# Scans that read ones from PSUM, and `1 - a` split between VectorE and GpSimd, in a hybrid decoder step

## The reference

```python
z = einsum('bqhd,bkhd->bhqk', q, k) * SB_HEAD_DIM ** -0.5 + bias
log_keep = where(vis, log_sigmoid(-z), 0)
after = cumsum(log_keep, reverse=True) - log_keep
a = where(vis, exp(log_sigmoid(z) + after), 0)
out = einsum('bhqk,bkhd->bqhd', a, v)
```

## Time and profile before

| | us |
|---|---|
| median of 3 runs | 2907.35 (2905.9 to 2910.66) |
| the profiled execution | 2908.15 |
| its span, first to last instruction | 2906.3 |
| TensorE busy in the span | 2503.2 |
| VectorE busy | 1422.4 |
| GpSimd busy | 1021.5 |
| ScalarE busy | 813.6 |

### The profile page before, as it was taken

How to read it: one execution, slowest core, us unless ns; L and a number is a source line. 1 busy time by engine, 2 the same in 40 slices (tenths; PEclk the granted TensorE clock), 3 DMA queues, 4 the chain that set the end, 5 groups by cost and what they waited for, 6 DMA issues and landing times. The chain is left out here.

```text
span 2906.3 us, 37872 instructions
## 1 busy us (share of the span) xinstructions
PE 2503.2 (86%) x14073; PEld 1568.7 (54%) x14073; DVE 1422.4 (49%) x1669; ACT 813.6 (28%) x1746; POOL 1021.5 (35%) x546
## 2 busy tenths in 40 slices
PE   5999899998599996999999667878888876886998
PEld 3555444443244443888888654555555554553443
DVE  1111066576100002555555319999999983442333
ACT  2222031223000001222222115656565642221110
POOL 2434010101000001435444005898898970002554
PEclk9999899999799997999999758999898998997999
DMA  5232212220522102011011121000000008994332
GB/s 155 90 96 92 47 30 45 61 60 15 93 64 70 59 31 65 27 39 43 29 43 33 46 99 64 30 30 1 30 30 1 30 1 291 330 325 164 127 127 83
DMA packets 150639, 224.91 MB, mean 77 GB/s; under 512 B 15632, under 2 KB 86241, under 8 KB 145416
## 3 DMA queue, kind: packets, MB, share of 16 engines
q1 hardware_dynamic: 150536, 223.50, 24.7%
HBM read 154.55 MB, written 68.91 MB: 77 GB/s over the span
## 5 line engine op out<-in xcount | busy, mean ns | idle before, releaser
L1561 DVE TENSOR_TENSOR_SCAN f_x<-f_x 128x2064 f32<-128x2064 f32 (+15 forms) x128 | 473.0, 3696 | 4.4
L1588 POOL TENSOR_TENSOR f_a<-f_a,f_x 128x2063 f32<-128x2063 f32 (+15 forms) x128 | 398.8, 3124 | 124.9 <-DVE f_x L1561 124.9
L629 PE MATMUL ps<-hT,wa 128*128 128x512 f32 (+1 forms) x960 | 354.4, 532 | 45.3 <-DMA wa<-w_in 45.3
L447 PE MATMUL ps<-hT,wc 128*128 128x512 f32 (+1 forms) x960 | 355.4, 532 | 12.8 <-DMA wc<-w_in 12.8
L629 PEld LDWEIGHTS ps<-hT,wa 128*128 128x128 f32 x960 | 168.7, 191 | 230.6 <-issue 185.1
L1456 PE MATMUL ps<-con,f_a 128*128 128x128 f32 x1216 | 189.7, 296 | 102.1 <-POOL f_a L1588 102.1
L447 PEld LDWEIGHTS ps<-hT,wc 128*128 128x128 f32 x960 | 169.1, 192 | 198.3 <-issue 198.3
L2010 PE MATMUL ps<-m_w,m_mT 128*128 128x512 f32 x544 | 238.1, 596 | 0.0
L321 PE MATMUL ps<-wt,hT_now 128*128 128x512 f32 x544 | 237.7, 595 | 0.0
L1511 ACT ACTIVATE f_at<-ps 128x512 f32<-128x512 f32 (+3 forms) x352 | 182.2, 539 | 197.6 <-PE ps L1456 195.2
L1456 PEld LDWEIGHTS ps<-con,f_a 128*128 128x128 f32 x1216 | 139.9, 149 | 138.7 <-POOL f_a L1588 108.7
(11 more groups left out here) (277 smaller groups left out, 3514.6 us busy)
## 6 DMA issues: line engine op xcount, KB each, us to landing
j_kp<-cache_k SPq DMA_DIRECT2D x128, 256.0 KB, 4.1
j_v<-cache_v SPq DMA_DIRECT2D x128, 256.0 KB, 4.7
chan<-y SPq DMA_DIRECT2D x12, 1088.0 KB, 6.0
chan<-ya SPq DMA_DIRECT2D x12, 1088.0 KB, 4.8
d_ld<-chan SPq DMA_DIRECT2D x16, 768.0 KB, 5.3
h_rows<-hg SPq DMA_DIRECT2D x17, 512.0 KB, 4.9
m_hh<-h_rows SPq DMA_DIRECT2D x17, 512.0 KB, 5.0
xin<-x_prompt SPq DMA_DIRECT2D x16, 512.0 KB, 4.1
```

What stands on the lines that cost most here:

```text
L447: m = pe.matmul(ps[:, ci, 0:n], wc[k][:, c, :], hT[:, c, c0:c0 + n], start=(c == 0), stop=(c == KC - 1))
L629: m = pe.matmul(ps[:, ci, 0:n], wc[k][h % 2][:, c, :], hT[:, c, c0:c0 + n], start=(c == 0), stop=(c == KC - 1))
L1561: dve.tensor_tensor_scan(dst[:, ::-1], dst[:, ::-1], dst[:, ::-1], 1.0, ALU.mult, ALU.bypass).then_inc(scanned, 1)
L1588: pool.tensor_tensor(w, w, x_at(u, h, i)[:, 1:], ALU.mult).then_inc(weighed, 1)
```

## The change

- A PSUM bank that nothing else writes (bank 7) gets a 1.0 in its first column, and `ones(n)` is that column, repeated n times. The value products move from bank 7 to bank 6.
- The transposes have two banks instead of three; `turn(t)` waits for the copy of turn t-2.
- The scan's unused operand is `ones(n)` instead of `x`, for both heads.
- The first head's `1 - a` stays on VectorE, but is a tensor_tensor: `ones(n)` minus `a`. The second head's moves to GpSimd, as the tensor_scalar that it was, in GpSimd's list ahead of the row's two products. It waits for the row's last sigmoid.
- `kept` becomes two semaphores, one per head. VectorE's second scan of a row waits for GpSimd's.

```diff
-        Z_BANK, T_BANK, O_BANK = 0, 4, 7
+        Z_BANK, T_BANK, O_BANK, ONE_BANK = 0, 4, 6, 7
+        def ones(n):
+            return ps[:, ONE_BANK, 0:1].broadcast_to([P, n])
...
-                if t >= 3:
-                    pe.wait_ge(evacuated, START + t - 2)
+                if t >= 2:
+                    pe.wait_ge(evacuated, START + t - 1)
...
             dve.memset(v[:, 0, :], 0.0).then_inc(filled, 1)
+            dve.memset(ps[:, ONE_BANK, 0:1], 1.0).then_inc(filled, 1)
...
+            dve.wait_ge(filled, START + 3)
...
                     for h in range(2):
-                        m = 4 * u + 2 * i + h
-                        if u >= 2 and i == 0 and h == 0:
-                            dve.wait_ge(weighed, START + 4 * (u - 1))
-                        dve.wait_ge(z_read, START + 2 * n - 1 + h)
+                        m = 2 * u + i
                         dst = x_at(u, h, i)
-                        dve.tensor_scalar(dst, a_at(u, h, i)[:, M0:], -1.0, 1.0, ALU.mult, ALU.add).then_inc(kept, 1)
-                        dve.wait_ge(kept, START + m + 1)
-                        dve.tensor_tensor_scan(dst[:, ::-1], dst[:, ::-1], dst[:, ::-1], 1.0, ALU.mult, ALU.bypass).then_inc(scanned, 1)
+                        if h == 0:
+                            if u >= 2 and i == 0:
+                                dve.wait_ge(weighed, START + 4 * (u - 1))
+                            dve.wait_ge(z_read, START + 2 * n - 1)
+                            dve.tensor_tensor(dst, ones(row_width(r)), a_at(u, h, i)[:, M0:], ALU.subtract).then_inc(kept[0], 1)
+                        dve.wait_ge(kept[h], START + m + 1)
+                        dve.tensor_tensor_scan(dst[:, ::-1], dst[:, ::-1], ones(row_width(r)), 1.0, ALU.mult, ALU.bypass).then_inc(scanned, 1)
...
                 if u < NU:
+                    n = chunk0[u]
                     for i, r in enumerate(unit_rows[u % UNITS]):
+                        n += len(row_chunks(r))
+                        pool.wait_ge(z_read, START + 2 * n)
+                        pool.tensor_scalar(x_at(u, 1, i), a_at(u, 1, i)[:, M0:], -1.0, 1.0, ALU.mult, ALU.add).then_inc(kept[1], 1)
                         for h in range(2):
```

More of the change, by code:

```diff
@@ L1370, in prompt_attention @@
     gate_loaded = p.sem("pgate_loaded")
-    z_acc, z_read, kept, scanned, weighed = p.sem("z_acc"), p.sem("z_read"), p.sem("kept"), p.sem("scanned"), p.sem("weighed")
+    z_acc, z_read, scanned, weighed = p.sem("z_acc"), p.sem("z_read"), p.sem("scanned"), p.sem("weighed")
+    kept = [p.sem("kept_first_head"), p.sem("kept_second_head")]
     turned, evacuated, av_done = p.sem("A_turned"), p.sem("AT_evacuated"), p.sem("av_done")
@@ L1451, in turn @@
                     pe.wait_ge(weighed, START + 4 * u + 2 * i + t % 2 + 1)
-                if t >= 3:
-                    pe.wait_ge(evacuated, START + t - 2)
+                if t >= 2:
+                    pe.wait_ge(evacuated, START + t - 1)
                 src = a_at(u, t % 2, i)
                 for j in range(min(4, r + 2 - 4 * g)):
-                    m = pe.transpose(ps[:, T_BANK + t % 3, j * P:(j + 1) * P], src[:, (4 * g + j) * P:(4 * g + j + 1) * P], p.ident)
+                    m = pe.transpose(ps[:, T_BANK + t % 2, j * P:(j + 1) * P], src[:, (4 * g + j) * P:(4 * g + j + 1) * P], p.ident)
                 m.then_inc(turned, 1)
@@ L1469, in values @@
                 m.then_inc(av_done, 1)
-            pe.wait_ge(filled, START + 2)
+            pe.wait_ge(filled, START + 3)
             for s in range(NU + LAG):
@@ L1510, in evacuate @@
                 nb = min(4, r + 2 - 4 * g) * P
-                act.activation(at[t % 4][:, 0:nb], ps[:, T_BANK + t % 3, 0:nb], ACT.Copy).then_inc(evacuated, 1)
+                act.activation(at[t % 4][:, 0:nb], ps[:, T_BANK + t % 2, 0:nb], ACT.Copy).then_inc(evacuated, 1)
             def outputs(u, n, i):
```

## The result

The changed kernel takes 2756.24 us (median of 4 runs, 2754.71 to 2756.97), against 2906.68 for the kernel before in the same comparison: a ratio of 0.9479, 95% interval 0.9463 to 0.9496. The forecast was 2762, in a range of 2740 to 2815. The profiled execution's span went from 2906.3 to 2755.1 us. From TensorE's first score to the end of its last value product, the stage took 659.0 us before (1737.05 to 2396.07) and takes 507.2 now (1736.13 to 2243.34).

The account below looks back on a forecast made before the run. VectorE, full, and GpSimd taking turns were held to bound prompt attention at 19.97 us a unit; with TensorE binding at 15.5, the stage ends at 2250.6 instead of 2396.1, so 2907.35 − 145.5 gives 2762 us, range 2740 to 2815.

Parts of the forecast that it names:

- Scan and product take turns: Prompt attention: VectorE's scan and GpSimd's product, each with two SBUF operands, exclude each other; a unit takes 19.97 us.
- rival 3: Prompt attention: the turns stay despite the PSUM operand; 20.8 to 26 us a unit, 25 to 180 us slower; 7%.
- The prices: Instruction costs in prompt attention without turns: VectorE 405 us in all, GpSimd 374 us.
- the copy's price: GpSimd's second-head `1 - a` costs what a one-operand copy does: 0.17 + 0.85n/1000 us, 71 us for 64.
- TensorE's unit: TensorE needs 15.43 us for a unit's work at full clock and becomes the bound; taken as 15.5.
- the long rows' chain: Units 0 and 1 of eight, with the longest rows, exceed TensorE's unit by 0.8 and 0.3 us.
- the two units of lag: The lag absorbs part of the 0.8 and 0.3 us by which units 0 and 1 exceed TensorE's unit.
- The pair's chain: VectorE and GpSimd's dependent instructions through a unit's two rows: 16.2 to 13.0 us, mean 14.5, close behind TensorE.
- The sum: Attention stage: step 2 at about 1759.5, 30 units of 15.5, last two steps 26.1; gain 145.5 us.
- Two banks: TensorE's transposes with two banks instead of three cost nothing, as long as ScalarE is not behind.
- the new waits: VectorE's second scan waits for GpSimd's `1 - a`, GpSimd for the second head's scores; counted within the pair's chain.
- Rival 1: GpSimd becomes the bound if its `1 - a` costs 3 us per 1000 columns: 17.8 a unit, about 2830 us; 14%.

Follow-up runs that it names:

- the second experiment: Changed kernel with the scan's second operand given as x in SBUF again, all else as changed: 2917.23 us, ratio 1.0026.
- the run where it binds: Changed kernel without the value products of the odd blocks of each group but a row's last, output incomplete: 2710.24 us, ratio 0.9315.
- the fourth: Kernel before with two transpose banks instead of three, nothing else: 2909.26 us, ratio 1.0001.
- the seventh experiment: Changed kernel with GpSimd's `1 - a` for the short row ahead of the long row's second product: 2754.43 us, ratio 0.9474.
- The first experiment: Kernel before with only the scan's unused operand from the PSUM ones, and so two transpose banks: 2756.6 us, ratio 0.9472.
- the third experiment: Changed kernel with the scan's unused operand from a repeated SBUF column of ones instead of PSUM: 2916.55 us, ratio 1.0024.
- the sixth experiment: Changed kernel with both heads' `1 - a` on VectorE as ones from PSUM minus a: 2762.62 us, ratio 0.9495.

## Why the prediction was right, point by point

- **What bound.** "Scan and product take turns" held, and its cause was the one given: the operand's memory. With the operand in SBUF again, the stage is at 20.2 us a unit (the second experiment: step 2 at 1764.07, step 32 at 2371.11), so rival 3's time of 20.8 to 26 was near for a kernel in which the turns stay, though somewhat dear.
- **The prices.** Scans: 321 us forecast, 310.2 measured; by shape 4.440 at 2064 columns and 0.454 at 144, or 0.155 + 2.076n/1000, so the fixed part was put too high by 0.085 and the price of 1000 columns too low by 0.026. The repeated PSUM element costs nothing extra: 2.308 at 2064, forecast 2.31, 82.4 us in all against 84. GpSimd's `1 - a` has the copy's price: 71.2 against 71. Products 273.6 against 274, gates 27.9 against 29.
- **TensorE's unit.** 15.43 from one stretch of the trace before, 15.33 measured. I added 0.07 for the long rows' chain; nothing was needed, since TensorE's matmuls wait for no product once step 2 has begun. That the two units of lag take it up is likely, but no run shows it.
- **The pair's chain.** Mean 14.5 forecast, 13.94 in the run where it binds. The term that failed is the chain's sum of durations: it had 0.03 (2064 columns) to 0.08 (144) too much in each scan, took an instruction to begin when the one ahead ends (two scans of 4.440 take 8.80, not 8.88), put 0.15 on each hand-over between the engines (0.08 from scan to product and 0.04 from `1 - a` to scan in the lines of the changed kernel's start), and gave the gate products 0.4 us in unit 7 that they don't take. It didn't matter, because TensorE's 15.33 lies above both.
- **The sum.** From the first score to step 2: 25.98 us before, 22.35 after, a gain of 3.6 (forecast 3.5). The 30 steps: 139.3 (forecast 134.2). The last two steps: 8.9 (forecast 7.7). Of the 139.3, 90.8 are idle time of TensorE that is gone (93.3 before, 2.6 now), and 48.6 are its own busy time, shorter at the higher granted clock (505.91 at 0.90, 457.35 at 0.99). Together 151.8, against 145.5; the 6 us between 2762 and 2756 are for the most part the 0.17 us a unit between 15.5 and 15.33.
- **Two banks and the new waits.** The banks were put at nothing, and the new waits at nothing beyond the pair's chain. Both held: the fourth and the seventh experiment, and the 457.35 of 459.92 us.
- **What it didn't see.** The prediction counted the PSUM form of `1 - a` and the split as parts of one change and gave neither a share of the gain. The first experiment shows that share to be nothing that can be measured. Only the form that has both on VectorE, at 1.04 ns a column, is a little slower.
- **A slip.** Rival 1's 6.87 us per 1000 columns is 6.82 by the prediction's own prices (3 + 2.05 + 1.77). Nothing hangs on it: GpSimd's `1 - a` measured 0.83 us per 1000, not 3.

The Trainium skill's SBUF — State Buffer, § Who interferes with whom, names the shared read port for a VectorE instruction with two SBUF inputs; the second and the third experiment agree with it (479.6 us of scans against 310.2). The other half of the prediction's reading, that one SBUF input doesn't take turns, holds for the subtraction from PSUM, but it is put too widely, and the trace of before doesn't agree with it: the tensor_scalar of before has one SBUF input, and the one below, of 144 columns, takes 3.80 us beside two products that run from 1911.94 to 1923.72, where another at 1758.98 took 0.20.

```profile
1916.22 3.80 DVE L1559 TENSOR_SCALAR f_x<-f_a 128x144 f32<-128x144 f32 x1
```

The forecast didn't suffer, since the changed kernel has no such instruction on VectorE in this stage. The first experiment has, and the last section names what the reading left out.

## What to carry to other kernels

When two engines are both nearly full and their instructions come out at sums of each other's durations, look at the memory of every operand first, also of one that the operation doesn't use: moving it can give more than sharing the work differently. The new wait on an engine that was no longer the bound cost nothing here, so look at what binds next before spending anything on one. And a dense stretch of the next engine in the trace of before was a good forecast of the new pace: 15.43 there, 15.33 here.

## What the runs showed of the hardware

- An operand that `bypass` leaves unused still makes the scan take turns with GpSimd when it lies in SBUF, even as one repeated element of another tile (0.45 us for 144 columns from PSUM, 3.71 with an SBUF operand beside a product).
- A tensor_scalar on VectorE with a single SBUF operand takes turns with GpSimd's products as well: 3.47 us for 144 columns. The Trainium skill's SBUF — State Buffer, § Who interferes with whom, names the two-port modes of such instructions as a second cause; the trace of the first experiment agrees with it, in the turns and in the pace (1.24 us for 2064 columns with nothing in the way, where the subtraction takes 2.31). The subtraction from PSUM shows none of it: 0.28 us for each of the sixth experiment's eight with 144 columns, also where a product runs all the while.
- Reading one PSUM element 2064 times costs what reading a row costs: 2.308 us, with 1.04 ns for each further column, against 2.31 and 1.043 by the prediction's line through the earlier trace rows.
